# Stick-breaking attention and its projections in one order of work on a Trainium2 core

## The reference, cut to what matters

```python
kv = (hk @ kv_w).reshape(B, S, 2, SB_HEADS, SB_DH)       # hk: normed with kv_norm, kv_mod
q = (h @ w_q).reshape(B, S, SB_HEADS, SB_DH)             # h: normed with norm_mix[1], mod
z = einsum('bqhd,bkhd->bhqk', q, k) * SB_DH ** -0.5      # 16 heads of 64, strictly causal
log_one_minus = where(causal, log_sigmoid(-z), 0)
tail = cumsum(log_one_minus, reverse) - log_one_minus
a = where(causal, exp(log_sigmoid(z) + tail), 0)
x = x + g_m * (einsum('bhqk,bkhd->bqhd', a, v) @ w_out)
```

## Time and profile before

| what | value |
|---|---|
| median of 3 runs | 1677.79 us (1676.78 to 1679.43) |
| span of the profiled execution, first to last instruction | 1675.8 us |
| PE busy, of the span | 93% |
| DVE busy, of the span | 84% |
| ACT busy, of the span | 65% |
| mean granted TensorE clock | 0.968 of full speed |

### The profile page before, as it was taken

The page is one execution under the profiler, slowest core; times in us unless marked ns, Lnnn a source line. Parts: engine busy times, 40 slices in busy tenths (PEclk is TensorE's granted clock), DMA queues, the critical chain, the costliest instruction groups (busy, mean ns, idle before and its releaser), DMA issues.

```text
span 1675.8 us, 22428 instructions
## 1 busy us (share of the span) xinstructions
PE 1565.9 (93%) x7164; PEld 1294.4 (77%) x7164; DVE 1405.6 (84%) x1537; ACT 1085.8 (65%) x1176; POOL 58.1 (3%) x47
## 2 busy tenths in 40 slices
PE   4999997999979676899999999999999999999996
PEld 4788775888768555788888888888888888888884
DVE  6889997788876444698998998998998998998995
ACT  3444434444454653687787777787787787787874
POOL 0212200000000120000000000000000000000000
PEclk9999998999989787899999999999999999999998
DMA  9977785888848102599999999999999999999991
GB/s 335 349 246 278 265 274 199 276 300 314 294 171 274 50 3 75 212 392 356 349 375 355 348 381 352 350 380 344 364 372 343 358 384 343 358 377 345 353 383 79
DMA packets 235113, 500.89 MB, mean 299 GB/s; under 512 B 9744, under 2 KB 40640, under 8 KB 235072
## 3 DMA queue, kind: packets, MB, share of 16 engines
q1 hardware_dynamic: 233904, 500.29, 82.6%
q10 hardware_dynamic: 1168, 0.07, 0.0%
HBM read 499.28 MB, written 1.05 MB: 299 GB/s over the span
## 4 chain that ended last, share of the span: by engine, by line
PE 81%; DVE 9%; DMA 3%; issue 3%; ACT 3%; POOL 1%; DVEq 0%; SPq 0%; ACTq 0%; POOLq 0%
PE ps L492 24%; PE ps L494 24%; PE ps L493 24%; DVE acc L1321 2%; DVE w_lo L1302 2%; DMA ada<-in_ada_w 2%; PE ps L866 1%; PE ps L767 1%; DMA raw<-in_ret_w_in 1%; PE ps L525 1%; DMA ada<-in_kv_ada_w 1%; PE ps L899 1%; PE ps L875 1%; PE ps L876 0%; PE ps L900 0%
## 5 line engine op out<-in xcount | busy, mean ns | idle before, releaser
L1302 DVE TENSOR_TENSOR w_lo<-raw,w_hi 128x1024 fp32r<-128x1024 f32 x834 | 990.9, 1225 | 100.2 <-ACT w_hi L964 86.2
L964 ACT ACTIVATE w_hi<-raw 128x1024 fp32r<-128x1024 f32 x834 | 864.5, 1058 | 246.3 <-PE ps L494 229.4
L492 PE MATMUL ps<-w_hi,RA 128*128 128x512 f32 x1560 | 618.1, 396 | 9.0 <-DVE w_lo L1302 2.9
L494 PE MATMUL ps<-w_hi,RA 128*128 128x512 f32 x1560 | 609.4, 391 | 0.0
L493 PE MATMUL ps<-w_lo,RA 128*128 128x512 f32 x1560 | 608.4, 390 | 0.0
L492 PEld LDWEIGHTS ps<-w_hi,RA 128*128 128x128 f32 x1560 | 293.7, 188 | 68.7 <-issue 3.4
L494 PEld LDWEIGHTS ps<-w_hi,RA 128*128 128x128 f32 x1560 | 293.4, 188 | 62.4
L493 PEld LDWEIGHTS ps<-w_lo,RA 128*128 128x128 f32 x1560 | 294.0, 188 | 59.4 <-issue 0.7
L492 PE MATMUL ps<-w_hi,hT_hi 128*128 128x512 f32 x432 | 172.6, 399 | 8.1 <-DVE hT_lo L1372 6.9
L494 PE MATMUL ps<-w_hi,hT_lo 128*128 128x512 f32 x432 | 170.2, 394 | 0.0
L493 PE MATMUL ps<-w_lo,hT_hi 128*128 128x512 f32 x432 | 170.1, 394 | 0.0
(11 more groups left out here) (220 smaller groups left out, 874.0 us busy)
## 6 DMA issues: line engine op xcount, KB each, us to landing
raw<-in_moe_w_in SPq DMA_DIRECT2D x224, 1024.0 KB
raw<-in_moe_w_out SPq DMA_DIRECT2D x112, 1024.0 KB
ada<-in_ada_w SPq DMA_DIRECT2D x46, 1024.0 KB, 7.3
raw<-in_ff_w_in SPq DMA_DIRECT2D x44, 512.0 KB
raw<-in_ret_w_in SPq DMA_DIRECT2D x16, 1024.0 KB
raw<-in_ff_w_out SPq DMA_DIRECT2D x11, 1024.0 KB
raw<-in_ret_w_in SPq DMA_DIRECT2D x16, 512.0 KB
raw<-in_ret_w_out SPq DMA_DIRECT2D x8, 1024.0 KB
```

Source lines behind the costliest of these rows:

```text
L492: pe.matmul(out, a_hi, b_hi, start=first, stop=False)
L494: return pe.matmul(out, a_lo, b_hi, start=False, stop=last)
L964: act.activation(w_hi[:, cn % RING, cols], raw[:, cn % RAW, cols], ACT.Copy).then_inc(hi_done, 1)
L1302: v.tensor_tensor(w_lo[:, cn % RING, cols], raw[:, cn % RAW, cols], w_hi[:, cn % RING, cols].bitcast(f32), ALU.subtract).then_inc(lo_done, 1)
```

## The change

- K and Q are projected transposed (`columns`): 128 weight columns are the stationary operand and the 256 tokens stream, so a tile is 8 input chunks x 4 column blocks x 3 passes = 96 matmuls of 256 columns, and the result is already in the layout of `kT`, `qT`. The `qk_t` buffers, their copies and the 32 transposes are gone.
- The order of weights becomes K, Q, V, output. V and output keep the old form (`token_rows`) and are cut in quarters of 12 matmuls, placed between `scores`, `tails` and `mix_values`. A step's scores and tails share two of four PSUM banks, so `scores(c)` waits for `log_weights(c - 2)`.
- ACT loads the table set `natural_log_exp_and_others` once ahead of the attention; Abs, Exp and Ln of a step stand together in `decline`.
- The conditioning's last 24 steps run two to a quarter, and are reduced by `reduce_last` and `mod_last` inside the new order.
- The first two quarters of the experts' weights are split before the second gate, not around `normed(3)`.

```diff
-U_SBO = U_Q + 4
+U_Q = U_KV + 4
+U_V = U_Q + 4
+U_SBO = U_V + 4
 U_MOE = U_SBO + 4
 MOE_U = 6 * ET
...
         def at_buf(c, n):
-            src = (FA[:, 6144:9216] if c % 2 == 0 else ada_flat[:, 0:3072])
-            off = (c // 2 % 2) * 1536 + n * 768
+            src = (FA[:, 6144:9216] if c % 4 < 2 else ada_flat[:, 0:3072])
...
-            halves += [(w, h, t * TW) for w in (sb_w_q[0], sb_w_out[0]) for t in range(2) for h in range(2)]
-            ada_after = {0: (22, 0), 1: (22, 1), 3: (23, 0), 4: (23, 1), 6: (24, 0), 8: (24, 1), 11: (25, 0), 13: (25, 1),
-                         15: (26, 0)}
+            halves = [(w, h, t * TW) for w in (kv_w, sb_w_q[0]) for t in range(2) for h in range(2)]
+            halves += [(kv_w, h, D + t * TW) for t in range(2) for h in range(2)]
+            halves += [(sb_w_out[0], h, t * TW) for t in range(2) for h in range(2)]
+            ada_after = {0: (22, 0), 1: (22, 1), 3: (23, 0), 4: (23, 1), 6: (24, 0), 7: (24, 1), 8: (25, 0), 9: (25, 1),
+                         10: (26, 0), 11: (26, 1)}
             for n, (w, h, col) in enumerate(halves):
                 load_half(U_KV + n, 0, w, h * 4 * P, col)
                 if n in ada_after:
                     load_ada(*ada_after[n])
-            load_ada(26, 1)
...
+            def columns(c, first, end, bank0, q, a_hi, a_lo):
+                for n in range(first, end):
+                    cn, s = c + n // 2, (c + n // 2) % RING
+                    pe.wait_ge(h_ok, 4 * q + n + 1)
+                    landed(cn, 0, n % 2)
+                    for t in (2 * (n % 2), 2 * (n % 2) + 1):
+                        kc = 4 * (n // 2) + t
+                        for k in range(4):
+                            wc = slice(t * TW + k * P, t * TW + (k + 1) * P)
+                            o = ps[:, bank0 + k // 2, (k % 2) * S:(k % 2 + 1) * S]
+                            pe.matmul(o, w_hi[:, s, wc], a_hi[:, kc, :], start=kc == 0 and k % 2 == 0, stop=False,
+                                      skip_group_check=True)
+                            pe.matmul(o, w_hi[:, s, wc], a_lo[:, kc, :], start=False, stop=False,
+                                      skip_group_check=True)
+                            last = pe.matmul(o, w_lo[:, s, wc], a_hi[:, kc, :], start=False, stop=kc == KC - 1,
+                                             skip_group_check=True)
+                    last.then_inc(w_used, 1)
+            def token_rows(c, n, bank0, step, a_hi, a_lo, kc0, first, last_one):
+                landed(c, 0, n)
+                for t in (2 * n, 2 * n + 1):
+                    cols = slice(t * TW, (t + 1) * TW)
+                    for b in range(NB):
+                        tok = slice(b * P, (b + 1) * P)
+                        last = passes(ps[:, bank0 + step * b, :], a_hi[:, kc0 + t, tok], a_lo[:, kc0 + t, tok],
+                                      w_hi[:, c % RING, cols], w_lo[:, c % RING, cols], first and t == 0,
+                                      last_one and t == 3)
+                last.then_inc(w_used, 1)
+            def values(t, n):
+                token_rows(U_V + 2 * t + n // 2, n % 2, 4, 1 + t, hT_hi, hT_lo, 4 * (n // 2), n < 2, n >= 2)
+            def out_rows(h, t, n):
+                token_rows(U_SBO + 2 * t + h, n, 4 + t, 2, oT_hi, oT_lo, 4 * h, h == 0, h == 1)
+            def reduce_last(u):
+                pe.wait_ge(ada_step, 8 * (u + 1))
+                bank = (2, 3, 7)[u - 24]
                 for c in range(4):
-                    for b in range(NB):
-                        last = pe.transpose(ps[:, bank + c // 2, (c % 2) * S + b * P:(c % 2) * S + (b + 1) * P],
-                                            qk_t[n % 2][:, b, c * P:(c + 1) * P], ident[:, :])
-                last.then_inc(kqT_done, 1)
-            pe.wait_ge(x_ok, 4)
-            tile(U_KV, 0, (4, 5), 2)
-            tile(U_KV + 2, 0, (6, 7))
-            pe.wait_ge(kv_ev, 1)
-            tile(U_KV + 4, 0, (4, 5))
-            pe.wait_ge(kv_ev, 2)
-            tile(U_KV + 6, 0, (6, 7))
-            pe.wait_ge(h_ok, 16)
-            reduce_ada(24, 2)
-            transpose_kq(0)
-            tile(U_Q, 0, (4, 5), 3, hq_hi, hq_lo)
-            pe.wait_ge(mod_ok, 25)
-            transpose_kq(1)
-            tile(U_Q + 2, 0, (6, 7), 3, hq_hi, hq_lo)
-            pe.wait_ge(kqT_ev, 1)
-            transpose_kq(2)
-            pe.wait_ge(kqT_ev, 2)
-            transpose_kq(3)
-            reduce_ada(25, 4)
-            reduce_ada(26, 5)
+                    last = pe.transpose(ps[:, bank, c * P:(c + 1) * P], acc[:, u % 2, c * P:(c + 1) * P], ident[:, :])
+                last.then_inc(acc_red, 1)
...
-                if c < 2:
-                    pe.wait_ge(kqT_ev, c + 3)
-                elif c == 2:
-                    pe.wait_ge(mod_ok, 27)
-                else:
-                    pe.wait_ge(u_ok, c - 2)
+                pe.wait_ge(kq_ev, 3 + c // 4)
+                if c == 1:
+                    pe.wait_ge(mod_ok, 26)
+                if c >= 2:
+                    pe.wait_ge(u_ok, c - 1)
                 for h in range(2):
                     r = slice(DH * h, DH * (h + 1))
-                    o = ps[:, 2 * (c % 3) + h, :]
+                    o = ps[:, 2 * (c % 2) + h, :]
                     pe.matmul(o[:, 0:S], kT[r, c, 0:P], qT[r, c, :], start=True, stop=True)
...
                 for h in range(2):
-                    o = ps[:, 2 * (c % 3) + h, :]
+                    o = ps[:, 2 * (c % 2) + h, :]
...
+            pe.wait_ge(x_ok, 4)
+            columns(U_KV, 0, 4, 4, 2, hT_hi, hT_lo)
+            columns(U_KV + 2, 0, 4, 6, 2, hT_hi, hT_lo)
+            pe.wait_ge(kq_ev, 1)
+            columns(U_Q, 0, 4, 4, 3, hq_hi, hq_lo)
+            reduce_last(24)
+            pe.wait_ge(kq_ev, 2)
+            columns(U_Q + 2, 0, 2, 6, 3, hq_hi, hq_lo)
             scores(0)
+            columns(U_Q + 2, 2, 4, 6, 3, hq_hi, hq_lo)
+            reduce_last(25)
             scores(1)
-            for g in range(KC // 2):
-                c = 2 * g
-                if c + 2 < KC:
-                    scores(c + 2)
-                if g:
-                    mix_values(c - 2)
-                    mix_values(c - 1)
-                tails(c)
-                tails(c + 1)
-                if c + 3 < KC:
-                    scores(c + 3)
-            mix_values(KC - 2)
-            mix_values(KC - 1)
-            broadcast_gate(2, diag2, 4)
+            pe.wait_ge(kq_ev, 3)
+            values(0, 0)
+            tails(0)
+            values(0, 1)
+            pe.wait_ge(kq_ev, 4)
+            reduce_last(26)
+            scores(2)
+            tails(1)
+            values(0, 2)
+            scores(3)
+            values(0, 3)
+            tails(2)
+            pe.wait_ge(kv_ev, 1)
+            values(1, 0)
+            mix_values(0)
+            mix_values(1)
+            scores(4)
+            tails(3)
+            values(1, 1)
+            mix_values(2)
+            scores(5)
+            tails(4)
+            values(1, 2)
+            mix_values(3)
+            scores(6)
+            tails(5)
+            values(1, 3)
+            pe.wait_ge(kv_ev, 2)
+            out_rows(0, 0, 0)
+            mix_values(4)
+            scores(7)
+            tails(6)
+            out_rows(0, 0, 1)
+            mix_values(5)
+            tails(7)
+            mix_values(6)
             pe.wait_ge(u_ok, KC)
+            broadcast_gate(2, diag2, 0)
+            mix_values(7)
             pe.wait_ge(ol_ok, KC)
...
+            out_rows(1, 0, 0)
+            out_rows(1, 0, 1)
+            for h in range(2):
+                out_rows(h, 1, 0)
+                out_rows(h, 1, 1)
+            broadcast_gate(3, diag3, 2)
+            pe.wait_ge(gbc_ev, 4)
             pe.wait_ge(x_ok, 6)
...
+            def kq_out(n):
                 act.wait_ge(w_used, before_half(U_KV + 2 * n + 2))
-                bank = 4 + 2 * (n % 2)
-                act.activation(dst, ps[:, bank:bank + 2, :], ACT.Copy).then_inc(kv_ev, 1)
-            def kq_out(n):
-                act.wait_ge(kqT_done, n + 1)
-                bank = 2 * (n % 2)
-                dst = (kT if n < 2 else qT)[:, 4 * (n % 2):4 * (n % 2) + 4, :]
+                bank, half = 4 + 2 * (n % 2), 4 * (n % 2)
+                dst = (kT if n < 2 else qT)[:, half:half + 4, :]
                 act.activation(dst.rearrange("p (n c) s -> p n (c s)", n=2), ps[:, bank:bank + 2, :], ACT.Copy,
-                               scale=1.0 if n < 2 else DH ** -0.5).then_inc(kqT_ev, 1)
-            split_quarters(U_KV, 0, 6, 9)
-            tile_out(0, v_all[:, :, 0:TW])
...
+                               scale=1.0 if n < 2 else DH ** -0.5).then_inc(kq_ev, 1)
+            def values_out(t):
+                act.wait_ge(w_used, before_half(U_V + 2 * t + 2))
+                act.activation(v_all[:, :, t * TW:(t + 1) * TW], ps[:, 4:6 + 2 * t:1 + t, :], ACT.Copy)\
+                   .then_inc(kv_ev, 1)
...
```

(132 more changed lines are left out.)

80 lines of the change are left out of this document (11 added, 69 removed).

## The result

The changed kernel takes 1656.2 us (median of 4 runs, 1654.26 to 1657.19) against 1678.6 (4 runs beside it, 1676.78 to 1682.88): ratio 0.9865, interval 0.9853 to 0.9877, 22.4 us less. The forecast was 1649.5, with a range of 1643 to 1663. The execution profiled took 1656.74 us, with a span of 1655.0.

A forecast was written before the change was run, and what follows sets the result against it. It took a chain across PE, ACT, DVE and POOL to pace the attention, with no engine full. Projection end 26.4 us earlier plus norm 2.1 gave 28.5 off 1677.8: 1649.3, say 1649.5 us; range 1643 to 1663.

The forecast's parts named there:

- p, the 256-column matmul, 0.118: K and Q projections on PE: each 256-column matmul takes 0.118 us, load and stream overlapping; four tiles take 45.3 us.
- the serial rival: In `columns`, each load waits for the matmul before it: p = 0.227, 41.9 us more, 1691 us; chance 7%.
- the load-record rival: In `columns`, loads pace at their record's length: p = 0.188, 26.9 us more, 1676 us; chance 4%.
- K and Q, E = start + 48.2: K and Q projections through `scores(0)`: slow clock 1.5, matmuls 45.3, reduction 0.5, `scores(0)` 0.9; E is their end, 525.5 us.
- E to `scores(2)`, 16.5, PE idle 5.9, 2.0 of slow clock: Start of the weave: `scores(2)` waits for DVE's queued `log_weights(0)`, ending at E+16.5; PE idles 5.9 us, slow matmuls add 2.0.
- `scores(2)` to the end of `scores(6)`, 29.5 + 2.0: Middle of the weave: PE sets the pace at 6.3 us a step, 29.5 us in all, plus 2.0 of slow clock.
- `scores(6)` to gate 3, 40.6, with a wait of 2.3: End of weave and output projection: 40.6 us, with a 2.3 us stall at the first output quarter.
- The norm 2.1 earlier: After the output projection: no expert quarter stands before `normed(3)`, so PE's transposes come 2.1 us earlier.
- The rival of DVE's order biting more often: In the weave, waits at `mod_last`, a softplus behind a quarter, or a lasting slow clock: 1662 us; chance 6%.
- The rival of the table loads: In the weave, ACT still loads tables before each Exp and Ln: about 10 us more, 1659 us; chance 5%.
- later stages keep their order and length: Stages after the changed region, experts included (about 1007 us), were carried over unchanged.
- start as before at 477.3: First projection matmul of the changed stage: starts at 477.3 us, as in the kernel before.

The follow-up runs named there:

- the second chip: The changed kernel run again unedited, on the chip of three of the follow-up runs: 1653.7 us, ratio 0.986.
- experiment 4: Changed kernel with `columns` streaming 192 of the 256 tokens, 384 matmuls as before: 1653.6 us, one execution; starts 0.111 us apart.
- experiment 1: Changed kernel with DVE's `log_weights(0)` and `softplus(1)` moved before quarter 21, `mod_last(26)` and quarter 22: 1647.0 us, ratio 0.9811.
- two traces: Changed kernel without the table set loaded ahead of the attention, run twice: 1658.6 us (ratio 0.9877) and 1658.4 us (ratio 0.9883).
- experiment 7: Experiment 1 plus the weave's end reordered on PE, ACT and DVE: 1640.3 us, ratio 0.9777; the same without the table loaded ahead: 1648.3 us, ratio 0.9817.
- experiment 3: Kernel before with only the common table set loaded ahead of the attention: 1678.7 us against 1678.8, ratio 1.000.
- experiment 6: Kernel before with K and Q projected transposed and one table set loaded early, without the weave: 1672.1 us, ratio 0.9958.

## Why the prediction was right

The mechanism is the forecast one: PE's gaps were filled, the slow clock went with them, and one stall of the forecast place and length was left. Each term of the forecast is given in italics, then what was measured. The hit in time is less sharp than in the stage. The median of 1656.2 lies at the edge of the forecast's own range (1643 to 1656) and falls into the stated range only because that was widened to 1663 for two rivals, neither of which came about. On the second chip the median is 1653.7, inside.

- *p, the 256-column matmul, 0.118*: 0.120, so 46.1 us for 384 in place of 45.3. Load and stream overlap; the serial rival (1691) and the load-record rival (1676) fall by the 0.120 itself, and experiment 4 shows that at 192 columns the load paces. The page "TensorE: Matmul & The Clock Gate" of the Trainium skill, section "Part 3: Packing small matmuls — row/col tiling", has a sentence that would put them one after the other; the measured 0.120 with full-array loads disagrees, and the measurement decides. The same section also says that a load which goes to a background weight buffer is pulled ahead of running matmuls; no run here tells whether that is what happens.
- *K and Q, E = start + 48.2*: 49.5 (481.20 to 530.66): 0.8 from p, the rest from a slower start (1.9 us of slow clock in place of 1.5, worked out in the same way). PE never waits up to `scores(0)`, so DVE keeps up, as forecast.
- *E to `scores(2)`, 16.5, PE idle 5.9, 2.0 of slow clock*: 16.2 and 5.66. The slow stretch is real, but experiment 1 prices it at 1.5 us rather than 2.0.
- *`scores(2)` to the end of `scores(6)`, 29.5 + 2.0*: 31.2. PE sets the pace, as the step's sum said.
- *`scores(6)` to gate 3, 40.6, with a wait of 2.3*: 41.0 and 2.12. Together E + 88.4 against E + 88.6: three terms, each within 0.5 us, whose misses (-0.3, -0.3, +0.4) partly cancel.
- *The norm 2.1 earlier*: 2.1 (10.1 to 8.0), read from the traces; no run moves the expert quarters alone.
- *The rival of DVE's order biting more often*: it didn't. Besides the stall, the longest wait for DVE in the weave is 1.1 us, at `scores(1)`, and the clock is back at 1.00 from 550 us on.
- *The rival of the table loads*: the loads went. The page "ScalarE: Activation LUTs" of the Trainium skill, section "Table sets: the hidden batching unit", has Exp and Ln in one set, and the single load at 508.40 agrees. The rival's price of 10 us was too high: 8.1 in two traces, 2.4 and 4.7 in their medians, 6.7 in experiment 7.
- *What was wrong*: of the 7.7 us by which the span lies above the forecast's 1647.3, only 1.0 is in the changed stage. The rest is the step "later stages keep their order and length" and, ahead of it, "start as before at 477.3". They kept their order, but their length varies by up to 4 us at the retention's end (228.8 to 233.1 over all traces; the changed stage begins at 477.0 to 482.1) and 2.5 in the last expert. The forecast took both from one execution in which both were short, so it stood below all of what the kernel shows (1649.95 to 1657.2 in 8 runs). Why the retention stage is late in some executions stays open: PE is idle 3.5 us there against 2.2 and its mean clock is 0.97 against 1.00, but what comes first wasn't tested.

## What to carry to other kernels

Where a chain over several engines leaves one idle in small gaps, put independent matmuls of about the length of a gap between the steps: it fills the gaps and keeps the clock up, and both count (here 16.5 us of idle time and an estimated 7.4 of slow matmuls). Taking work off the chain without filling the gaps gave nothing in experiment 3 and at most 3 us in experiment 6, while in the weave the same edit is worth several microseconds. After weaving, read every engine's queue for an operation that waits for something late while another engine needs what stands behind it: here one such place cost 7 us, and reordering both ends of the weave took 9.6 us off the stretch from the last of `columns` to gate 3 (88.4 to 78.8), and 13.4 off the median on the same chip.

## What was not expected of the hardware

- At 256 columns load and stream are balanced: 0.120 us for a pair, 0.111 at 192 columns, 0.2267 at 512. Below 256 columns a narrower stream bought next to nothing: 0.111 at 192 and 0.113 at 8.
- Where waits were shortened but not removed (experiments 3 and 6), gate 2 and the start of the projection ran at 0.50, and the projection took 26.0 us in place of 23.6. The router's transposes then met the full level and took 1.94 us in place of 3.43. The mean clock of the attention stayed at 0.72 and 0.73. Why the slow stretches moved as they did wasn't tested.
- The last tile of the last expert ran at the slow level in some executions (0.63 us a matmul) and not in others (0.39) of the same kernel, 2.5 us apart.
